# Block 3 of a three-block kernel: the order of its projections, and one filler stream through the stick-breaking attention

## The reference

```python
h = layer_norm_3(x, ln_in_g, ln_in_b)
proj = h @ w_in                     # 1024 x 2304: q, k, v of 8 "stick" heads, q of 8 sliding heads, 2 k and 2 v heads
# stick-breaking attention, 8 heads of 64, strictly causal:
z = q @ k.T * scale
A[t,s] = sigmoid(z_ts) * prod_{s<j<t} (1 - sigmoid(z_tj));  out = A @ v
# sliding window attention, window 128, grouped queries, a sink and a relative bias per head:
p = softmax over (previous block, own block) of (q @ k.T * scale + bias), with the sink in the sum;  out = p @ v
merged = concat(rms_norm_3(sb_out), rms_norm_3(swa_out));  mix = merged @ w_out
```

## Time and profile before

| | us |
|---|---|
| median of three runs | 2956.73 |
| lowest, highest | 2954.72, 2958.47 |
| profiled execution | 2955.75 |
| its span, first to last instruction | 2954.4 |
| TensorE busy in it | 2857.5 (97%) |
| VectorE, ScalarE busy | 1931.6 (65%), 1306.4 (44%) |

### The profile page before, as it was taken

One profiled execution on the slowest core, in us unless ns is written; L12 is line 12 of the kernel. 1 busy time (PEld: TensorE's weight loads), 2 busy tenths in 40 slices (PEclk: granted clock), 3 DMA queues, 4 the chain that ended last, 5 costly groups with the idle time before them and its releaser, 6 DMA issues.

```text
span 2954.4 us, 35689 instructions
## 1 busy us (share of the span) xinstructions
PE 2857.5 (97%) x14306; PEld 2224.7 (75%) x14306; DVE 1931.6 (65%) x2891; ACT 1306.4 (44%) x2069; POOL 13.3 (0%) x15
## 2 busy tenths in 40 slices
PE   8999999999999998999999999999999999999998
PEld 6787777788888886777775777665567788888886
DVE  5443439776777777876784674667767755555575
ACT  4223425434443446454546444555644433233335
POOL 0000000000000000000000000000000000000001
PEclk9999999999999999999999999999999999999999
DMA  4211111111111111111010110000001111111112
GB/s 160 77 57 43 36 50 36 57 43 57 50 58 50 53 55 43 37 43 43 30 36 23 43 43 29 30 15 29 23 29 50 38 49 58 58 43 58 57 51 79
DMA packets 49986, 141.73 MB, mean 48 GB/s; under 512 B 12918, under 2 KB 16798, under 8 KB 49694
## 3 DMA queue, kind: packets, MB, share of 16 engines
q1 hardware_dynamic: 49822, 139.45, 15.0%
HBM read 135.16 MB, written 9.77 MB: 49 GB/s over the span
## 4 chain that ended last, share of the span: by engine, by line
PE 80%; DVE 10%; ACT 6%; issue 4%; POOL 0%; DMA 0%; SPq 0%; DVEq 0%; ACTq 0%; POOLq 0%
PE psum L985 24%; PE psum L608 14%; PE psum L1063 13%; PE psum L1259 11%; PE psum L641 3%; PE psum L750 2%; PE psum L1344 1%; PE psum L1371 1%; PE psum L724 1%; PE psum L1191 1%; PE psum L681 1%; PE psum L1170 1%; PE psum L798 1%; DVE y L3205 1%; PE psum L745 1%
## 5 line engine op out<-in xcount | busy, mean ns | idle before, releaser
L2466 ACT ACTIVATE w_hi<-w_raw 128x512 fp32r<-128x512 f32 x280 | 175.0, 625 | 317.3 <-DVE w_raw L3796 188.9
L3063 DVE TENSOR_TENSOR residual<-residual,psum 128x1024 f32<-128x1024 f32 x160 | 194.4, 1220 | 122.3 <-PE psum L1063 122.3
L985 PE MATMUL psum<-h_hi,w_hi 128*128 128x512 f32 x640 | 249.2, 389 | 2.7 <-ACT mlp_ta L2392 2.6
L985 PE MATMUL psum<-h_hi,w_lo 128*128 128x512 f32 x640 | 249.0, 389 | 0.0
L985 PE MATMUL psum<-h_lo,w_hi 128*128 128x512 f32 x640 | 248.9, 389 | 0.0
L608 PE MATMUL psum<-h_hi,w_hi 128*128 128x512 f32 x688 | 220.0, 401 | 4.2 <-DVE w_lo L2547 4.2
L3827 DVE TENSOR_TENSOR w_lo<-w_raw,w_hi 128x512 fp32r<-128x512 f32 x280 | 192.4, 687 | 35.3 <-ACT w_hi L2466 35.0
L608 PE MATMUL psum<-h_hi,w_lo 128*128 128x512 f32 x688 | 212.2, 390 | 0.0
L608 PE MATMUL psum<-h_lo,w_hi 128*128 128x512 f32 x688 | 212.2, 390 | 0.0
L1063 PE MATMUL psum<-mlp_act_hi,w_hi 128*128 128x512 f32 x640 | 198.6, 392 | 6.1 <-DVE residual L3063 4.1
L1259 PE MATMUL psum<-h_hi,w_lo 128*128 128x512 f32 x576 | 201.6, 412 | 0.0
(11 more groups left out here) (476 smaller groups left out, 5645.1 us busy)
## 6 DMA issues: line engine op xcount, KB each, us to landing
w_raw<-in_weights SPq DMA_DIRECT2D x228, 512.0 KB, 3.6
residual<-in_x_t SPq DMA_DIRECT2D x8, 512.0 KB, 9.6
out_t<-residual SPq DMA_DIRECT2D x16, 256.0 KB, 2.1
rel_copies<-rel_rows SPq DMA_DIRECT2D x8, 480.0 KB, 5.8
na_bias<-rel_copies SPq DMA_DIRECT2D x8, 240.0 KB, 4.5
band_copies<-band_rows SPq DMA_DIRECT2D x8, 192.0 KB, 6.2
ret_rotary<-in_rotary SPq DMA_DIRECT2D x1, 1024.0 KB, 12.5
swa_bias<-band_copies SPq DMA_DIRECT2D x4, 256.0 KB, 2.8
```

The lines of the kernel that those rows point to most:

```text
L985: ins = self.pe.matmul(out[bank[j]], w[:, k, :], x(k), start=(j in emptied and k == 0 and part == 0), stop=(k == 3 and part == 2), skip_gr ...
L2466: ins = self.act.activation(dst, src, ACT.Copy)
L3063: self.dve.tensor_tensor(x, x, self.m.place["down", t, n], ALU.add).then_inc(*self.to("dve_down", t, n))
```

## The change

Tiles change places. The triple behind the norm now makes the values, keys and queries of stick pair 0 (banks 2, 0 and 4). The two tiles that followed it are gone from that place; only the transposes of the values stay. All other tiles, 13 of them, form one stream through all four pairs: v, k, q of pairs 1 to 3, the sliding values (`KV_T`), the sliding keys (`KV_K`), the sliding queries of pairs 0 and 1. It is fed 12 matmuls ahead of step 0, then 2 + 4 + 6 in every stick step; 6, 6 and 6 between the first sliding steps, and the 18 that are left in sliding steps 2 to 4. The fillers of the sliding steps are 4 + 4 from step 7 and 5 + 5 from step 17; the mean moves from step 13 to 15. The copies and the splits of weights move with the tiles on ScalarE and VectorE. Cut to its core:

```diff
-    return B3 + 14 + p if name == "wq" else B3 + 2 + 3 * p + ("v", "k", "q").index(name)
+    return B3 + 14 + p if name == "wq" else B3 + 3 * p + ("v", "k", "q").index(name)
+KV_T, KV_K = B3 + 12, B3 + 13
...
 TensorE, kv:
-        self.project_triple("l1", (("act_k2",), ("act_kvt",), ("act_svraw", 0)),
+        self.project_triple("l1", (("act_svraw", 0), ("act_sk", 0), ("act_sq", 0)),
...
-        for n, (first, emptied) in enumerate(((6, ("act_sk", 0)), (2, ("act_sq", 0)))):
...
+        q.wait_ge(*on("act_svraw", 0))
+        self.transposes(self.take(("pe_svtok", 0), 6, 2, ("act_svtok", 0)), m.svraw).then_inc(*to("pe_svtok", 0))
...
 TensorE, attention:
+        evicted = [one for p in range(1, PAIRS) for one in (("act_svraw", p), ("act_sk", p), ("act_sq", p))]
+        evicted += [("act_kvt",), ("act_k2",), ("act_wq", 0), ("act_wq", 1)]
+        rest = self.background([(B3 + 3 + n, (2, 0)[n % 2], told) for n, told in enumerate(evicted)])
         self.q.wait_ge(*self.on("dve_sb_consts"))
+        self.run(rest, 12)
...
             self.run(rest, 2)
             if d:
                 self.stick_turn(2 * d - 2)
-            self.run(rest, 4 if p < PAIRS - 1 else 2)
+            self.run(rest, 4)
             if d:
                 self.stick_turn(2 * d - 1)
-            self.run(rest, 8 if p < PAIRS - 1 else 3)
+            self.run(rest, 6)
...
+        self.q.wait_ge(*self.on("act_k2"))
         self.window_scores(0)
         self.run(rest, 6)
         self.stick_turn(2 * end - 2)
-        for _ in rest:
-            pass
+        self.run(rest, 6)
         self.window_scores(1)
         self.stick_turn(2 * end - 1)
+        self.run(rest, 6)
         self.stick_out(end - 1)
...
+            if step == 7:
+                rest = self.background([(sb_tile("wq", 2), 2, ("act_wq", 2))])
...
+            elif step == MEAN + 2:
                 rest = self.background([(sb_tile("wq", 3), 2, ("act_wq", 3))])
...
+            filling = 4 if step < MEAN else 5
...
 ScalarE, attention:
+            last = p == PAIRS - 1
+            if e == 3:
+                self.window_values() if last else self.stick_values(p + 1)
+            elif e == 5:
+                self.window_tokens() if last else self.stick_tokens(p + 1)
             elif e == 7:
+                self.window_keys(0) if last else self.stick_keys(p + 1)
+            elif e == 11:
+                self.queries("wq", 0) if last else self.queries("q", p + 1)
+            if last and 8 <= e < 11:
+                self.window_keys(e - 7)
+            if e % 4 == 3:
+                self.split_up_to(B3 + 5 + d // 4)
...
-        q.wait_ge(*on("pe_sz", PAIRS - 1, len(STICK) - 1))
-        self.queries("wq", 1)
-        self.split_up_to(sb_tile("wq", 3))
...
+            if step == 6:
+                q.wait_ge(*on("pe_sz", PAIRS - 1, len(STICK) - 1))
+                self.queries("wq", 1)
+                self.split_up_to(sb_tile("wq", 3))
...
 VectorE, attention:
-        self.split_up_to(B3 + 6)
+        self.split_up_to(B3 + 4)
...
+            if d and e % 4 == 0:
+                self.split_up_to(B3 + 4 + d // 4)
...
             if step == 5:
+                self.split_up_to(sb_tile("wq", 2))
+            elif step == 9:
                 self.split_up_to(sb_tile("wq", 3))
-            elif step == 12:
+            elif step == 16:
                 self.split_up_to(B3 + 18)
-            elif step == 24:
+            elif step == 26:
                 self.split_up_to(B3 + 19)
-            if 15 <= step < 15 + 2 * 4:
+            if 17 <= step < 17 + 2 * 4:
```

More of the change, by code:

```diff
@@ L711, in project_triple @@
         for half, s in halves():
-            outs = [self.take(("triple", t + j, half), 2 * j + half, 1, emptied[j]) for j in range(2)]
+            outs = [self.take(("triple", t + j, half), (2, 0)[j] + half, 1, emptied[j]) for j in range(2)]
             for k in range(KD):
@@ L715, in project_triple @@
                     if (k, j) == (0, 2):
-                        outs.append(self.take(("triple", t + j, half), 2 * j + half, 1, emptied[j]))
+                        outs.append(self.take(("triple", t + j, half), 4 + half, 1, emptied[j]))
                     self.q.wait_ge(*self.on("w_lo", t + j))
@@ L1299, in attention @@
                 self.transposes(out, m.svraw).then_inc(*self.to("pe_svtok", p + 1))
+            elif e == VTOK:
+                self.q.wait_ge(*self.on("act_kvt"))
+                out = self.take(("pe_kvT",), own, 2, ("act_v2",))
+                self.transposes(out, m.svraw).then_inc(*self.to("pe_kvT"))
+        self.q.wait_ge(*self.on("act_k2"))
         self.window_scores(0)
@@ L1311, in attention @@
                 self.window_scores(step)
-            if step == MEAN:
+            if step == 7:
+                rest = self.background([(sb_tile("wq", 2), 2, ("act_wq", 2))])
+            elif step == MEAN:
                 self.q.wait_ge(*self.on("dve_sacc", PAIRS - 1, STICK_DONE[-1]))
@@ L1315, in attention @@
                 self.means(out, "mean512", m.n6_acc, "pe_n6_mean")
+            elif step == MEAN + 2:
                 rest = self.background([(sb_tile("wq", 3), 2, ("act_wq", 3))])
-            elif step >= 3 and step != MEAN + 1:
-                self.run(rest, 3 if step < MEAN else 4)
+            filling = 4 if step < MEAN else 5
+            if step != MEAN:
+                self.run(rest, filling)
             if TURN <= step < PAIRS * NCH + TURN:
                 self.window_turn(step - TURN)
-            if step >= 3 and step not in (MEAN, MEAN + 1):
-                self.run(rest, 3 if step < MEAN else 4)
+            self.run(rest, filling)
             if step >= OUT:
@@ L2218, in kv, with window_values, window_tokens, window_keys @@
     def kv(self):
[L2219 to L2226, removed]
         self.stick_values(0)
+        self.stick_keys(0)
+        self.queries("q", 0)
         self.split_up_to(B3 + 4)
[L2229 to L2232, removed]
         self.stick_tokens(0)
-        self.queries("q", 0)
-        self.split_up_to(B3 + 6)
+    def window_values(self):
+        self.q.wait_ge(*self.on("proj", KV_T))
+        self.act.activation(self.m.svraw, self.m.place["proj", KV_T], ACT.Copy).then_inc(*self.to("act_kvt"))
+    def window_tokens(self):
+        m = self.m
+        self.q.wait_ge(*self.on("pe_kvT"))
+        self.act.activation(m.v2[:].rearrange("p n d -> p (n d)"), m.place[("pe_kvT",)], ACT.Copy).then_inc(*self.to("act_v2"))
+    def window_keys(self, part):
+        g, a = divmod(part, 2)
+        self.q.wait_ge(*self.on("proj", KV_K))
+        ins = self.act.activation(self.m.k2[64 * a:64 * a + 64, g, :], self.m.place["proj", KV_K][64 * g:64 * g + 64, :], ACT.Copy)
+        if part == 3:
+            ins.then_inc(*self.to("act_k2"))
     def stick_values(self, p):
@@ L2299, in attention @@
                 self.window_out(step - OUT)
-            if step == 11:
+            if step == 6:
+                q.wait_ge(*on("pe_sz", PAIRS - 1, len(STICK) - 1))
+                self.queries("wq", 1)
+                self.split_up_to(sb_tile("wq", 3))
+            elif step == 13:
                 q.wait_ge(*on("pe_wscore", 0, NCH - 1))
@@ L3459, in attention @@
             if step == 5:
+                self.split_up_to(sb_tile("wq", 2))
+            elif step == 9:
                 self.split_up_to(sb_tile("wq", 3))
-            elif step == 12:
+            elif step == 16:
                 self.split_up_to(B3 + 18)
-            elif step == 24:
+            elif step == 26:
                 self.split_up_to(B3 + 19)
-            if 15 <= step < 15 + 2 * 4:
-                k, half = divmod(step - 15, 2)
+            if 17 <= step < 17 + 2 * 4:
+                k, half = divmod(step - 17, 2)
                 cut = slice(half * HALF, half * HALF + HALF)
```

68 lines of the change are left out of this document (10 added, 58 removed).

## The result

The changed kernel takes 2940.76 us (median of 4 runs, 2939.64 to 2942.10), the kernel before beside it 2955.72 (4 runs): ratio 0.9949, 95% interval 0.9936 to 0.9961. That is 15.0 us less, where 10.3 were forecast; the time lies 0.24 us under the range of 2941.0 to 2952.5. The direction and the places were right. The idle time of the stick steps was taken too small, and one place was not looked at.

A forecast was written before the change was run, and what follows sets the result against it. TensorE is busy 2857.5 of 2954.4 us, so the change can only remove its waits. Terms -12.95 - 1.4 + 4.3 + 0.3 - 1.55 + 1.0 = -10.3 us gave 2946.4 us, range 2941 to 2952.5.

The forecast's parts named there:

- Parts 1, 2: Block 3's start and stick steps: idle of 13.25 us goes, less 0.3 for short waits, gain 12.95.
- part 6: Clock: slow stretch between pairs 1 and 2 goes, gain 1.55; new wait before sliding step 7 may bring one, loss 1.0.
- part 1: Start of stick pair 0: the 1.2 us wait for `sq` goes; pair 0's extra idle of 1.09 is inside the 13.25.
- Part 3: Sliding steps 0 to 3: their 1.39 us of idle goes, gain 1.4.
- Part 4: Sliding steps 5 to 7 lose cover: waits of 1.6 in step 5 and 2.7 before step 7's first filler, loss 4.3.
- Part 5: Sliding steps 13 to 17 repeat the old pattern of 11 to 15; idle at the end rises, loss 0.3.
- rival B: Sliding steps take back next to nothing, the bank coming with 1 us of wait: 2942.1 us, chance 0.14.
- Rivals A: Sliding steps take back more, VectorE lagging and the clock falling in 5 to 7 and once more: 2951.9, chance 0.14.
- C: Slower: ScalarE late in stick steps, a whole copy in front costing 0.46 a step, 22 us over 48: 2968, chance 0.04.
- D: Stream isn't one: each of 13 tiles waits 0.4 for bank or weights at its start, 5.2 us: 2952, chance 0.06.

The follow-up runs named there:

- seven: Changed kernel with 7 fillers a step in stick pair 3 and the other 60 in one block after it: 2947.66 us, ratio 0.9971.
- gaps_back: Changed kernel with the old run-out in all four stick pairs (14 fillers a step, 4 in step 10, none in step 11): 2955.28 us, ratio 0.9992.
- again: The changed kernel, unaltered, run and profiled once more: 2940.89 us, ratio 0.9944.
- no_cover: Changed kernel with stick-step fillers placed 2, 10, 0 for 2, 4, 6, none between second transposes and output product: 2970.23 us, ratio 1.0048.

## Why the prediction was right or wrong

**Parts 1, 2 and the gain in part 6, the failed step.** They gave 12.95 + 1.55 = 14.5 us. Measured were 20.4, and every place was as said: no wait in any stick step, none for `sq`, the clock at the border of pairs 1 and 2 at 1.00. The step that failed is "taking the length less TensorE's busy time as its idle time", 13.25 us. This counts only what sticks out behind modelled ends; that these overlap the next matmul stood beside the profile of the kernel before, and the sum left it out. The stick steps alone gained 19.3 us: 264.06, and 13.60 for 60 more fillers and 1.02 for eight transposes that moved in, less 259.36. The other 1.1 lie in front of them. The missing 5.9 us are:

- 5.2 hidden in the stick steps, found by holding the kernel before against the changed one matmul for matmul: 0.7 in pair 0 (67.75 - 63.35 longer, 67.75 - 64.06 = 3.69 shown), 1.3 in pairs 1 and 2 (140.08 - 130.71, 6.56 shown, 1.55 slow clock), and 3.2 in pair 3 (56.23 against 65.30 - 13.60 - 1.02 = 50.68; 2.32 shown). Pair 3 of the changed kernel is the first row below. `seven` has most of that last loss again, in the changed kernel;
- 0.3 charged for short waits and not needed, since the margin was 0.74 and not 0.55;
- 0.4 in front of the first scores (1.1, less the 0.68 that the sum did count). The stretch of pair 0 was cut at 1799.00, in the middle of the wait for `sq` (second row, the kernel before), which began at 1799.68 - 1.21 = 1798.47. So 0.53 us of this wait were never in the 13.25, though part 1 has it "inside"; another 0.4 of pair 0's surplus of 1.09 was a wait for `sb_beta`.

```profile
1973.71:2039.01 65.30, 65.30 (x434) 45.03 (x432) 46.35 (x80) 39.79 (x83) 0.00 (x0) 1.00 0.12 33
```

```profile
1799.68 0.49 PE L1344 MATMUL psum<-sb_k,sb_q 64*128 64x128 f32 x4 [1.21 <-ACT sb_q L2254]
```

The 1.55 for the clock came, but that the change brought it is not shown: `gaps_back` has the run-out at the end of all four pairs and no slow stretch, and in the one profile of the kernel before only one of three such borders has one. This term may be luck.

**Part 3** was right: no idle in steps 0 to 3.

**Part 4** had both waits in their places: 1.6 forecast and 1.39 found in step 5, 2.7 and 2.02 ahead of step 7. 0.9 too much.

**Part 5** took steps 13 to 17 as they were and 0.3 more at the end. At the clock of the kernel before, which `again` has in the last stretch, it came out close: 1.84 us idle in steps 13 to 21 (2.75 before in 11 to 20) and 34.37 - 24.47 = 9.90 in the last stretch (9.47 before), 0.5 less in all.

```profile
2114.81:2149.18 34.37, 24.47 (x197) 15.16 (x195) 28.38 (x115) 23.82 (x65) 0.00 (x0) 0.90 0.05 16
```

The 8.30 us of idle in the first profile (clock 0.81) are no gain. The same matmuls are busy 2.3 us longer there, but the stretch is only 0.7 us longer, for 1.6 of it lie where TensorE was idle in `again`.

**Part 6, the loss.** 1.0 was charged for a slow stretch behind the wait. Where it comes it costs 1.5; it came in five of seven profiles with the wait and in none of three without. The last stretch, said to stay at 0.90, was 0.81 here and 0.90 in `again`. All in all the sliding steps lost 3.1 us (2.4 in `again`) where parts 3 to 6 had 4.2: -1.4 + 4.3 + 0.3 + 1.0. The whole time came near rival B's 2942.1, but by luck: B had next to nothing lost in the sliding steps (-1.4 + 1.3), and its gain in the stick steps was as much too small as the forecast's. The rule on transposes of the Trainium skill ("TensorE: Matmul & The Clock Gate", Part 4: PE-mode transpose) did not show: steps 4 to 6, full of them, kept 1.00 in every profile of the changed kernel and its variants, and in steps 4 to 12 the clock fell only behind the wait.

**Not seen at all:** the 1.3 us at MLP 3. The diff showed the new order of banks in a function that MLP 3 also calls, and I followed it in block 3 alone.

The sum with measured terms, for the change run again: -20.1 (stick steps and start, by the same working), +2.4 (sliding steps), +1.3 (up to MLP 3) and +1.3 (from MLP 3 on, chance as above) are -15.1; its span is 15.2 less than that of the kernel before. Rivals A, C and D did not come: a whole stream of 13 tiles ran without one wait for a bank or for weights in the stick steps. C's price has its mechanism in `no_cover`: 0.44 us a step for each 0.45 taken from the cover, from the point where the cover is used up.

## What to carry to other kernels

The idle time of TensorE that this profile shows was a lower bound in every stretch compared here, so compare the step that waits with one that doesn't, matmul for matmul, and take the difference of lengths. Filler work is worth most when it is spread so thinly that it never runs out, and an even spread can be tried before any tile is moved. A wait for a bank is best looked for one step up on the engine that empties it, since one moved line gave 3.5 us here; and an edit in a shared helper has to be followed to each of its callers.

## What the runs showed of the hardware

- The shown idle falls short of the lost time by the modelled tail of the instruction in front: 0.16 us between a 128x512 matmul and transposes, 0.07 between it and the output product, and about 0.03 right behind transposes (1.6 us over the 47 waits of `no_cover`).
- One wait of 2.0 us was followed in five of seven profiles by a stretch at 1.2 GHz that cost 1.5 us, while 47 waits of 0.6 us, one every 6 us (`no_cover`), left the clock at 1.00. In the kernel before, one of three run-outs with waits of 0.8 and 1.1 us close together was followed by one, and none of the four in `gaps_back`: what decides it is open.
- In the last sliding stretch a clock of 0.81 in place of 0.90 added 2.3 us to TensorE's busy time and only 0.7 to the length, since TensorE waits there anyway.
- The clock from the block's triple to the first stick scores was 0.92 to 0.96 in kernels that don't differ up to there, and the stretch 1.3 us longer or shorter for it: a difference of this size in a single run needs a second profile before it is explained.
